# Hybrid attention block on one core: projections as Strassen products, intermediates in DRAM, attention in a stage of its own

## The reference, cut to what matters

```python
u = rmsnorm(h, g_pre)
qa, ka, va, za, qf, kf, vf, zf, ff, ga, gf = split(u @ w_in)      # widths 512,128,128,512, 512,512,512,512, 8, 1024,1024
y_swa = swa(qa, ka, va, sinks) * silu(za)    # 8 query heads, 2 key heads of 64; window of chunks, ALiBi, sinks, 16 meta keys
c     = cumsum(log_sigmoid(ff + b_forget))   # per head
p     = softmax(qf @ kf.T / 8 + c[t] - c[s], causal)              # 8 heads of 64, all earlier tokens ("FoX")
y_fox = (p @ vf) * silu(zf)
m     = sigmoid(ga + b0) * (y_swa @ w_up_swa) + sigmoid(gf + b1) * (y_fox @ w_up_fox)
out   = h + rmsnorm(m @ w_out, g_post)       # meta rows dropped
```

## Time and profile before

| | us |
|---|---|
| median of three runs | 933.11 (933.0 to 934.03) |
| the profiled execution | 933.41 |
| its span, first to last instruction | 931.6 |
| PE busy in it | 901.2 |
| mean granted clock of TensorE | 0.996 |

### The profile page before, as it was taken

The page is one execution under the profiler, slowest core; times in us unless marked ns, Lnnn a source line. Parts: engine busy times, 40 slices in busy tenths (PEclk is TensorE's granted clock), DMA queues, the critical chain, the costliest instruction groups (busy, mean ns, idle before and its releaser), DMA issues.

```text
span 931.6 us, 15521 instructions
## 1 busy us (share of the span) xinstructions
PE 901.2 (97%) x6084; PEld 784.7 (84%) x6084; DVE 388.2 (42%) x1089; ACT 355.3 (38%) x790; POOL 234.9 (25%) x181
## 2 busy tenths in 40 slices
PE   4999999999999999999999999999999999999995
PEld 3999988899888998889988888888888888878995
DVE  7956556544465453654646624010010011062133
ACT  6435555354444453543634415111111211252332
POOL 4344222032211122211230112332232233220132
PEclk9999999999999999999999999999999999999998
DMA  9063211032200151100330011111111112125053
GB/s 284 5 105 87 53 24 46 13 104 47 58 19 17 46 115 23 47 24 24 92 69 24 1 46 45 46 46 46 46 46 45 46 46 59 54 78 170 1 182 114
DMA packets 82762, 56.91 MB, mean 61 GB/s; under 512 B 24041, under 2 KB 76522, under 8 KB 82690
## 3 DMA queue, kind: packets, MB, share of 16 engines
q1 hardware_dynamic: 76258, 44.47, 17.5%
q0 software_dynamic: 4992, 7.18, 4.2%
q10 hardware_dynamic: 1440, 4.26, 1.2%
HBM read 44.50 MB, written 4.23 MB: 52 GB/s over the span
## 4 chain that ended last, share of the span: by engine, by line
PE 92%; DVE 4%; DMA 2%; ACT 1%; issue 1%; DVEq 0%; SPq 0%; ACTq 0%
PE PS L1257 24%; PE PS L1259 22%; PE PS L1258 22%; PE PS L1383 7%; PE PS L1369 6%; PE PS L1346 3%; PE PS L1347 2%; PE PS L1377 1%; PE PS L1447 1%; PE PS L1279 1%; DMA y<-in_x_dram 1%; DVE kk_s L1139 1%; PE PS L1299 1%; DMA w_raw_slots<-in_w_in_dram 0%; DMA w_raw_slots<-in_w_out_dram 0%
## 5 line engine op out<-in xcount | busy, mean ns | idle before, releaser
L1257 PE MATMUL PS<-u_hi,w_hi_slots 128*128 128x256 f32 (+4 forms) x1008 | 328.8, 326 | 1.2 <-DVE w_low_slots L1047 1.2
L1258 PE MATMUL PS<-u_lo,w_hi_slots 128*128 128x256 f32 (+4 forms) x1008 | 321.2, 319 | 0.0
L1259 PE MATMUL PS<-u_hi,w_low_slots 128*128 128x256 f32 (+4 forms) x1008 | 320.8, 318 | 0.0
L1257 PEld LDWEIGHTS PS<-u_hi,w_hi_slots 128*128 128x128 f32 x1008 | 190.1, 189 | 19.9 <-issue 6.0
L787 POOL TENSOR_TENSOR w_low_slots<-w_raw_slots,w_hi_slots 128x1024 fp32r<-128x1024 f32 x49 | 119.1, 2430 | 337.5 <-ACT w_hi_slots L859 337.5
L1258 PEld LDWEIGHTS PS<-u_lo,w_hi_slots 128*128 128x128 f32 x1008 | 189.8, 188 | 11.9
L1259 PEld LDWEIGHTS PS<-u_hi,w_low_slots 128*128 128x128 f32 x1008 | 189.7, 188 | 11.5
L859 ACT ACTIVATE w_hi_slots<-w_raw_slots 128x1024 fp32r<-128x1024 f32 (+1 forms) x51 | 53.3, 1045 | 149.6 <-DMA w_raw_slots<-in_w_in_dram 112.3
L1209 DVE SCALAR_TENSOR_TENSOR gated<-tanh_g,PS 128x512 f32<-128x512 f32 x32 | 21.9, 686 | 200.9 <-PE PS L1259 200.9
L951 ACT ACTIVATE p_t<-PS 128x512 f32<-128x512 f32 (+2 forms) x104 | 55.2, 559 | 59.3 <-PE PS L1369 58.8
L1383 PE MATMUL PS<-p_t,v_f 128*64 128x128 f32 x576 | 58.4, 288 | 0.0
(11 more groups left out here) (185 smaller groups left out, 1443.3 us busy)
## 6 DMA issues: line engine op xcount, KB each, us to landing
w_raw_slots<-in_w_in_dram SPq DMA_DIRECT2D x33, 512.0 KB, 3.8
neg_c<-neg_c_dram SPq DMA_DIRECT2D x8, 520.0 KB, 6.2
x_again<-in_x_dram SPq DMA_DIRECT2D x8, 512.0 KB, 4.3
y<-in_x_dram SPq DMA_DIRECT2D x7, 512.0 KB, 6.8
w_raw_slots<-in_w_in_dram SPq DMA_DIRECT2D x14, 256.0 KB, 3.7
out_dram<-result ACTq DMA_DIRECT2D x6, 512.0 KB, 3.4
qq_s<-qq_s POOLq DMA_DIRECT2D x8, 256.0 KB, 3.9
qq_f<-qq_f POOLq DMA_DIRECT2D x8, 256.0 KB, 4.6
```

The costliest lines, as they stand in the source:

```text
L1257: pe.matmul(dst, w_hi[s][:, k, :], hi, start=first, stop=False)
L1258: pe.matmul(dst, w_hi[s][:, k, :], lo, start=False, stop=False)
L1259: return pe.matmul(dst, w_low[s][:, k, :], hi, start=False, stop=last)
```

## The change: what it does

Three phases that need different layouts of SBUF are separated, and what one makes for another is stored in DRAM (`k_dram`, `q_dram`, `v_dram`, `z_dram`, `g_dram`, `k_windows`) by SP and read back.

1. **Plain stage.** The forget gate, all keys and all values are projected as before, in chunks of 272 and 256 tokens. High and low parts of the keys and transposed values go through a ring of four `stage_a` slots to DRAM. DVE and ACT make four sums of blocks of `u` (`t_hi`, `t_lo`).
2. **Product stage.** The 32 blocks of queries, z and gates are taken in 16 couples. Tokens (512 + 512), width (512 + 512) and the couple's two blocks make 2 x 2 times 2 x 2, done in 7 products by Strassen's scheme in Winograd's form instead of 8; each product is 4 k-tiles x 3 matmuls of 128x512. DVE makes four weight sums for each couple (`weight_sums`) and folds the results out of PSUM; ACT and POOL split each operand in high and low part (9 slots); ACT drains (scale, tanh); SP stores.
3. **Attention stage.** Fox logits are made with keys on partitions and up to 512 queries along the row (`tile`), so that the exponential can be multiplied with the values without a transpose. The row maximum must then be known beforehand: `max` makes the logits once more, high part with the high and low parts of the keys stacked in one contraction of 128, with queries on partitions, DVE reduces them (`tensor_tensor_reduce` to `junk`), and the maxima come back as a row by a product with the identity (`row`), copied by ACT into free rows of `QB`. The gates of the keys are the exponential's bias. Row sums are made by POOL (`acc`, one 128-partition add for each tile and head) and a product with ones (`den`), then DVE's reciprocal of 128 columns four times. The swa items are as before, without the third product; POOL scales them. Score, max, row, trans and den share PSUM banks 0 and 1, fox logits banks 2 to 4.
4. **Merge and output.** Merge as before, with gates from DRAM. The output product has tokens on partitions (`m_hi` stationary, rows of w_out moving), so the transposes and `o_t` go.

The diff replaces most of the file; its core, from the new file:

```diff
+def products():
+    out = []
+    for p in range(N_COUPLES + 1):
+        if p < N_COUPLES:
+            out.append((p, "A11"))
+        if p:
+            out += [(p - 1, "S4"), (p - 1, "A22")]
+        if p < N_COUPLES:
+            out += [(p, "S2"), (p, "S1"), (p, "A12"), (p, "S3")]
+    return out
+def key_tile(q, i):
+    r0 = max(BANK * q, P * i - N_META if i else 0)
+    w = BANK * (q + 1) - r0
+    keys = min(P, LENGTH - P * i)
+    shift = r0 - (P * i - N_META)
+    masked = min(P - shift, w) if shift < P else 0
+    return r0, w, keys, masked, shift
...
+            # DVE, before each couple
+                link(nc.vector.tensor_tensor(s1, a21, a22, ALU.add))
+                link(nc.vector.tensor_tensor(s2, s1, a11, ALU.subtract))
+                nc.vector.tensor_tensor(s3, a11, a21, ALU.subtract).then_inc(sums_ready, 1)
+                nc.vector.tensor_tensor(s4, a12, s2, ALU.subtract).then_inc(sums_ready, 1)
...
+            # SP, after product S3 of the last couple: queries, kk_s from k_windows, v_a, v_b
+            # POOL queue, after product A12 of the last couple
+                pool.wait_ge(product_done, at[N_COUPLES - 1, "A12"] + 1)
+                stage_b_stored(pool, Q_USES)
+                stage_a_stored(pool, count_a["stage"])
+                load_fox(pool, 0)
+                pool.wait_ge(product_done, at[N_COUPLES - 1, "S3"] + 1)
+                pool.wait_ge(neg_c_stored, 16)
+                load_neg_c(pool, 0)
...
+            # PE
+                elif kind == "max":
+                    for x, (c0, w) in enumerate(st["pieces"]):
+                        masked = x == len(st["pieces"]) - 1
+                        for h in range(2):
+                            ms_wait(pe, k + h)
+                            ins = pe.matmul(PS[:, MS_BANK + (k + h) % 2, 0:w], QA[n][:, h, tok],
+                                            KA[n][:, h, c0:c0 + w], start=True, stop=not masked)
...
+                elif kind == "tile":
+                    for h in range(2):
+                        x = 2 * u + h
+                        dst = PS[0:keys, S_BANK + x % S_RING, 0:w]
+                        if x >= S_RING:
+                            pe.wait_ge(fox_exp, x - S_RING + 1)
+                        pe.matmul(dst, KA[n][:, h, kk], QA[n][:, h, tok], start=True, stop=False)
+                        ins = pe.matmul(dst, KB[n][:, h, kk], QB[n][:, h, tok], start=False, stop=not masked)
...
+                elif kind == "values":
+                    for h in range(2):
+                        x = 2 * u + h
+                        pe.wait_ge(fox_exp, x + 1)
+                        ins = pe.matmul(PS[h * HEAD:(h + 1) * HEAD, Y_BANK + f % 2, c0:c0 + w],
+                                        VF[j % 2][0:keys, i, h * HEAD:(h + 1) * HEAD],
+                                        p_fox[0:keys, x % PT_RING, 0:w], start=st["first"], stop=st["last"])
...
+                elif kind == "out":
+                        pe.matmul(dst, m_hi[:, k, tok], hi, start=k == 0, stop=False)
+                        pe.matmul(dst, m_hi[:, k, tok], lo, start=False, stop=False)
+                        ins = pe.matmul(dst, m_lo[:, k, tok], hi, start=False, stop=k == KT - 1)
...
+            # DVE
+                elif kind == "rec":
+                    nc.vector.reciprocal(den_row[:, cols], den_row[:, cols]).then_inc(rec_done, 1)
-                        ins = pe.transpose(PS[:, 4 + 2 * (n % 2) + d // 4, (d % 4) * P:(d % 4 + 1) * P],
-                                           o_t[:, g % 2, d, t * P:(t + 1) * P], ident[:, :])
```

More of the change, by code:

```diff
@@ L31 @@
 KT = D_MODEL // P
+HK = KT // 2
 NQ = SEQ // P
+NK = NQ + 1
 BANK = 512
@@ L263, in schedule @@
-    steps += [Step("natural", n=x, half=1) for x in range(n0, n0 + n)] + [
-        Step(kind, n=x) for kind in ("root", "finish") for x in range(n0, n0 + n)]
-    timed, seen = [], 5
-    for st in steps:
-        if st.entry is not None and st.kind != "split_w" and st.entry > 2:
-            while seen < len(entries) and seen <= st.entry + (2 if st.kind == "out" else 1):
-                timed.append(Step("split_w", entry=seen))
-                seen += 1
-        timed.append(st)
-    steps = timed
@@ L350, in schedule @@
-    steps = woven
-    return entries, steps, owner, totals
-def groups_of(st):
-    return st.groups if st.kind in ("values", "open") else []
+            steps.append(dict(kind="u_norm", n=m))
+        steps += [drain(x) for x in last]
+        last = now
+        steps += [dict(kind="split_w", entry=e) for e, turn in enumerate((1, 3, 4, 9)) if turn == m]
+    steps += [drain(x) for x in last]
+    sums = [("val", 0, 0), ("val", 0, 1), ("val", 0, 2), ("hi", 0), ("val", 2, 0), ("val", 2, 1), ("val", 2, 2),
+            ("hi", 2), ("val", 1, 0), ("val", 1, 1), ("hi", 1), ("val", 3, 0), ("val", 3, 1), ("hi", 3), ("lo", 0),
+            ("lo", 2), ("lo", 1), ("lo", 3)]
@@ new lines, in plain_steps, with pieces_of @@
+    assert not sums
+    return steps, count
+def products():
[8 more added lines that the diff above has]
+    return out
+def pieces_of(t):
+    n = t + 1
+    k = -(-(N_META + P * n) // BANK)
+    per = sorted(n // k + (1 if x < n % k else 0) for x in range(k))
+    out, at = [], 0
+    for x, c in enumerate(per):
+        w = P * c + (N_META if x == 0 else 0)
+        out.append((at, w))
+        at += w
+    return out
@@ new lines, in merge_steps @@
+def merge_steps():
+    order = [(0, 0, 0), (0, 0, 1), (1, 0, 0), (1, 0, 1), (0, 1, 0), (0, 1, 1), (1, 1, 0), (1, 1, 1)]
+    for d in range(2, KT):
+        order += [(d, b, c) for c in range(2) for b in range(2)]
+    steps, pairs = [], {}
+    for n, (d, b, c) in enumerate(order):
+        steps.append(dict(kind="up", d=d, b=b, c=c, n=n))
+        if b == 1:
+            pairs[d, c] = len(pairs)
+            steps.append(dict(kind="merge", d=d, c=c, n=pairs[d, c]))
+        if (b, c) == (1, 1) and d + 2 < KT:
+            steps.append(dict(kind="split_up", d=d + 2))
+        if (b, c) == (1, 0) and 2 <= d < 2 + HK:
+            steps.append(dict(kind="split_out", k=d - 2))
+    steps += [dict(kind="split_out", k=k) for k in range(HK, KT)]
+    for n in range(NQ):
+        steps.append(dict(kind="out", n=n))
+    return steps, {x: n for n, x in enumerate(order)}, pairs
@@ L358, in build @@
 def build(nc, x, meta_tokens, g_pre, w_in, b_forget, b_gate, sinks, w_up_swa, w_up_fox, w_out, g_post,
           ident_in, const_in, rows_in, out):
-    entries, steps, owner, totals = schedule()
-    items_done_groups = {}
-    for st in steps:
-        if st.kind == "open":
-            items_done_groups[st.i] = st.groups[-1]
+    steps_a, count_a = plain_steps()
+    prods = products()
+    at = {x: i for i, x in enumerate(prods)}
+    steps_c, ms_uses, units = attention_steps()
+    steps_d, up_number, merge_number = merge_steps()
```

2427 lines of the change are left out of this document (1431 added, 996 removed).

## The result

The changed kernel takes 1069.45 us (1067.88 to 1074.29, 4 runs) against 933.27 (4 runs) before: a ratio of 1.147, 95% interval 1.143 to 1.151. The prediction said 909, in a range of 877 to 958. It was wrong in direction, and the time lies outside that range.

A forecast was written before the change was run, and what follows sets the result against it. TensorE's issue time was taken to bound the kernel. From 931.6 us, -44.5 for products, -232 and +188 for attention, +28 bank waits, +18 loads, +4 clock and smaller terms gave 907.4; forecast 909, range 877 to 958.

The forecast's parts named there:

- the prediction's own signs of being wrong: Attention stage: over 255 us, granted clock under 0.9, or TensorE waiting for ACT or POOL would show the forecast wrong.
- Strassen products: Product stage: 1536 matmuls of 512 columns become 1344, 44.5 us less, with side engines' work beside TensorE.
- the rival of products that do not shrink: Product stage: side engines hold the products, 909 + 44 = 953 us; chance 0.04.
- Part 3: Parking in DRAM: before attention TensorE idles 18 us (8 to 33) for 8.2 MB at 306 GB/s.
- The rival of slow loads: Pause before attention: loads at the lower rate take 41.6 us, so +15, total 924, still faster; chance 0.12.
- Part 2: Attention in a stage of its own: the old 232 us removed, TensorE's own work there put at 188 us.
- the floor nor the ceiling of that bound: Attention's value products of 512 columns: 32 us taken; floor 16 if weight load holds, ceiling 64 if heads cannot overlap.
- 3 + 3 for tails and reciprocals: Attention: 3 us for POOL in the last pair (0 to 8), 3 us for reciprocals (0 to 16).
- 0.13 per use: Attention: forecast wait for each of 216 uses of PSUM banks 0 and 1; from 0.24 the gain is gone.
- the argument against the rival: Against two-bank waits deciding attention (75 us instead of 28, total 964, chance 0.12): tiles and values separate most uses.
- the clock rival: Small attention gaps hold TensorE at 1.2 GHz; decides from 28 of 188 us, 965 at 60; chance 0.10.
- the two slow rivals: Attention: waits on PSUM banks 0 and 1 (964, chance 0.12); TensorE at 1.2 GHz (965, chance 0.10).

The follow-up runs named there:

- late_and_z: Changed kernel with the loads of the gates' halves held until the first window score and a next pair's maxima begun two units later: 1046.94 us (1.1218).
- three_banks: Changed kernel with a third bank for the shared ring, taken from the tiles' ring, order of work unchanged: 1015.72 us (1.0883).
- before_bunched: Kernel before the change, with the projection pieces woven into attention all placed at one item of each run of eight: 1096.82 us, one run.
- three_banks_split: Changed kernel with a third shared bank, maxima pieces spread over the unit, row behind the values, next pair's maxima two units later: 1002.64 us (1.0743).
- warm_uses: Changed kernel with 160 filler matmuls of 464 columns in the pause and one ahead of each of 216 shared-bank waits: 1053.27 us (1.1281).
- three_banks_warm: three_banks_split with 160 filler matmuls in the pause and one ahead of a ring-bank use, only from a unit's values on: 1002.09 us (1.0727).
- warm_start: Changed kernel with 160 filler matmuls of 464 columns into an unused bank during the pause before attention: 1075.45 us, one run.
- split_max: Changed kernel with the pieces of a maxima step spread over the unit, nothing left out and no bank added: 1071.70 us (1.1483).

## Why the prediction was wrong

Three terms for the attention stage failed. The waits on the two shared banks were put at 28 us, and TensorE waited 57.5 us for VectorE's reductions. The loads of later pairs were called hidden, and cost 24. The clock was charged 4 us for the pause alone, and was low for 207 us, by an estimate some 60 us. Two of the prediction's own signs of being wrong came true: attention of 366 us, over 255, and a granted clock of 0.71 in it, under 0.9. Its third sign, ACT or POOL as what TensorE waits for, did not become the main wait.

By stage, against the sum of 907.4 for a span that came out at 1066.1:

- **Strassen products: right.** 1344 matmuls in 307.5 us, 0.229 each, no gap in 308 us. Neither POOL nor VectorE held them; the rival of products that do not shrink is out. The 44.5 us of gain are there.
- **Plain stage: 12 us too low.** The terms for start, forget gate, ten projections, value transposes and turn make 158; it took 170. The sums of the tokens were said to lag a few us; VectorE is 2.97 of 3 and 5.97 of 6 us busy where TensorE stands:

```profile
105.00:108.00 3.00, 1.12 (x10) 0.94 (x9) 2.97 (x3) 0.00 (x0) 0.00 (x0) 1.00 0.00 0
111.00:117.00 6.00, 1.22 (x6) 0.93 (x5) 5.97 (x4) 3.16 (x3) 4.12 (x1) 0.78 0.07 21
```

  TensorE waits 1.9 and 4.8 us there. The longer wait ends on a weight block: ScalarE rounds it at 111.2, behind its copy of a token sum that had waited for VectorE, and POOL's part is done at 116.5. After the first wait the clock falls, and from 108.6 to 122 us products start at about half their rate (256 columns each 0.21 us in place of 0.12). The prediction had charged this clock nowhere.

- **Exposed loads, Part 3: 18 predicted, 34.4 in the pause.** Bytes were right, the rate was 237 GB/s and not 306, and TensorE got no overlap from the last 8.3 us of products. Beyond that, "later loads are hidden" failed: 24.1 us of waits in three places, because the maxima of a next pair came only two units behind the issue of their keys. In the stretch shown above the running pair's first tile is at 654.1, TensorE has come to the next pair's maxima at 662, and they start at 672.9; a load of KB landed 11.6 to 16.6 us after its issue. Two units more were not enough to end the wait (17.0 us left in late_and_z). The rival of slow loads named the rate and missed this.
- **TensorE's own work in attention, Part 2: right.** The prices held. A pair of value products of 512 columns takes 0.91 us from its start to the next instruction where that is a sum of denominators, and 1.01 where it is a logit product, where 0.87 and 0.36 of switching were taken: neither the floor nor the ceiling of that bound applies, and the switching was priced too high here. The own columns, priced start to start at full clock, make by my count some 147 us against 188 less 45 of switching, 143.
- **The waits: 28 predicted, and 3 + 3 for tails and reciprocals.** TensorE was forecast to be idle for 25 to 40 us of the stage; it was idle for 103. Of the 366 us my count leaves 159 for waits and switches where the sum had 45 + 28 + 3 + 3: 57.5 on reductions, 24 on loads, 19 on other engines, and the rest in switches and gaps too short for the view of waits. One shared bank more gave back 54 us, some 24 of it idle time. The step that failed for the reductions is the arithmetic of 0.13 per use: it put the row and the transpose behind it at 0.4 together, while the row alone waited 0.85 on average, 28 times out of 32, and it charged a piece for VectorE's rate (0.54 a reduction) but not for its latency. A bank's turn took 1.2 us in the unit shown, product, hand-over, reduction and hand-over back, and VectorE's fixed queue has score reductions and reciprocals in it too. "Tiles and values stand between most uses" was the argument against the rival, and the waits shown above occur between pieces and before the row, where nothing stands between.
- **The clock: 4 predicted, on the pause alone.** It was low for 207 of 366 us. By my count the stage's own work took 119 us in that time and would take half at full clock, so the clock cost some 60 us, just the condition of the clock rival. This is an estimate and not a measured difference; TensorE's busy time in the low stretches, short waits included, is about 147 us (44.65 in the opening, 103 in the body by windows of 1 us), so 74 would be its ceiling. That the opening would be low was priced only as the upper end of the term (25). One reading behind the term was loose as well: 0.71 at the end of the kernel before is the mean of the four us after TensorE stopped, not the clock at their end. The prediction gave the two slow rivals a chance of 0.12 and 0.10 as if they excluded each other. They share a mechanism: bank waits make pauses in which the clock falls, as waits for loads do, and three_banks moved waits and low time with one edit. The Trainium skill, TensorE: Matmul & The Clock Gate, "A second HAM failure mode", which the prediction cited as a rival, says that small idles between groups that cycle through banks make the clock fall and rise; the trace agrees, with 0.76 in the body at 71% busy, and 0.83 with a third bank.
- **Reciprocals:** 0.4 taken, 0.92 measured for 128 columns. As copies they gave back 9.7 us (one run) against a term of 3, inside its bounds of 0 to 16. The Trainium skill, VectorE: DVE Perf Modes, section on the fixed hardware budget, gave an estimate of 1.1 by its repeat of 8: nearer than the row-based guess, a fifth too high. Its sum, some 10 us higher, would have been the better one here.
- **Merge and output:** from 878.8 on 187 us against about 193 in the sum; right, and 6 us on the cheap side.

Together 12 - 4.5 + 16 + 140 - 6 = 158 of the 159 us, where 140 is the stage of 366 against a predicted 226 (188 + 28 + 3 + 3 + 4). By the counts above these 140 are some 56 of clock, 30 of reductions, 24 of loads, 13 of other engines, and 17 of small gaps and own work. The deeper fault lies ahead of the terms. The prediction said itself that a wait of another engine is hidden only while projection matmuls stand in front of it, and then priced the uncovered stage with rates taken from the covered one. How large that cover was, before_bunched suggests: 166 us with one table of the kernel before changed.

What stays open: how the 69 us that three_banks_split has over the kernel before divide. The pause (34 us) and the waits named in its rows (22 and 17 us) would make 73, but they overlap with low clock, and no run took them away. No run held the clock full with the work unchanged, so its price alone is bounded only from below: at least 16 us with two banks (warm_uses). With three banks fillers gained nothing (three_banks_warm), which does not bound it, since they cost time too. Shortening the pause was tried in one way only, which missed. No version beat the kernel before.

## What to carry to other kernels

When a change moves latency-bound work out from under dense work, price it by round trips (fill, hand over, reduce, hand back) and not by rates, and try a bank ring with one slot more than the number of results that go out together (here three banks for two heads; no other size was tried). Where a saving in matmuls comes with the loss of a weave, first measure the old kernel without its weave. Waits and clock were not rival causes here: a stage with many small waits is better priced with part of its own work at half speed.

## What the runs showed of the hardware

- 160 back-to-back products kept the granted clock at 1.00 through 34 us, and it was 0.52 over the next 60 us of real work with TensorE 74% busy (warm_start). A body with one filler ahead of each bank wait had 0.85 in place of 0.76.
- The pause's reloads from DRAM, at a DMA share of 1.04 to 1.06, ran at 231 to 242 GB/s in all twelve kernels that have it, where the start of the kernel before had 306.
- Spreading the pieces without a free bank gained nothing (split_max, +2 us), a bank without reordering gained 54 us. The later start (late_and_z) did gain 22 us with two banks.
